# adaLN modulation in quarters, with packed weights and full-row score matmuls, in a hybrid SSD, MLA and PEER layer

## The reference

```python
ada = jnp.dot(jax.nn.silu(c), w_ada) + b_ada
shift1, scale1, gate1, shift2, scale2, gate2 = jnp.split(ada[:, None, :], 6, axis=-1)
h = layer_norm(x) * (1 + scale1) + shift1
z, xbc, dt_raw, q_a, kv_a, k_r, g_logits = jnp.split(jnp.dot(h, w_in), IN_OFFSETS, axis=-1)
...
scores = jnp.einsum('bqhd,bkhd->bhqk', q_blk, k).astype(jnp.float32) * scale
```

## Time and profile before

| | us |
|---|---|
| three runs | 3086.29, 3083.02, 3086.70 |
| median | 3086.29 |
| profiled execution, device time | 3086.24 |
| profiled execution, span of its instructions | 3084.3 |
| busy: PE, DVE, ACT, POOL | 1835.4, 2372.8, 684.8, 982.0 |
| low starts on PE (first matmul of unit 0) | 142.3 |
| att starts on PE | 209.6 |
| first gathered row used by DVE in PEER | 1709.3 |

### The profile page before, as it was taken

The page is one execution under the profiler, slowest core; times in us unless marked ns, Lnnn a source line. Parts: engine busy times, 40 slices in busy tenths (PEclk is TensorE's granted clock), DMA queues, the critical chain, the costliest instruction groups (busy, mean ns, idle before and its releaser), DMA issues.

```text
span 3084.3 us, 31543 instructions
## 1 busy us (share of the span) xinstructions
PE 1835.4 (60%) x10751; PEld 1496.0 (49%) x10751; DVE 2372.8 (77%) x2628; ACT 684.8 (22%) x712; POOL 982.0 (32%) x727
## 2 busy tenths in 40 slices
PE   1299999899999999999879221222222122122222
PEld 1288888888888888999769110111111010011111
DVE  7855556778878786444565898989898999999997
ACT  1143333234444444433343000000000000000000
POOL 0000001122222221000000555655554456666552
PEclk8598888999999999999989666566666556656666
DMA  7845556875666664655544999999999799999996
GB/s 271 308 148 162 167 176 207 286 222 191 209 207 201 202 213 159 239 184 185 210 144 131 376 404 416 392 401 391 403 389 407 309 403 406 418 404 400 404 405 266
DMA packets 255655, 880.19 MB, mean 285 GB/s; under 512 B 19496, under 2 KB 56976, under 8 KB 188208
## 3 DMA queue, kind: packets, MB, share of 16 engines
q0 software_dynamic: 93600, 614.51, 49.8%
q1 hardware_dynamic: 161872, 264.11, 25.9%
q10 hardware_dynamic: 64, 0.07, 0.0%
HBM read 876.49 MB, written 2.13 MB: 285 GB/s over the span
## 4 chain that ended last, share of the span: by engine, by line
PE 40%; DVE 29%; DMA 12%; issue 10%; POOL 5%; ACT 2%; SPq 0%; DVEq 0%; POOLq 0%; ACTq 0%
DVE ps L1822 10%; DMA rrow<-in_peer_u,eid 10%; PE ps L595 9%; PE ps L597 9%; PE ps L596 9%; POOL rrow L1956 5%; DVE acc L1312 4%; DVE rrow L1795 4%; PE ps L575 2%; PE ps L576 2%; PE ps L577 2%; DVE wlo L1256 2%; ACT whi L938 2%; DMA rrow<-in_peer_v,eid 1%; PE aux L794 1%
## 5 line engine op out<-in xcount | busy, mean ns | idle before, releaser
L918 PE MATMUL aux<-rrow,acc 128*128 128x512 f32 x512 | 333.6, 817 | 1021.5 <-DVE acc L1815 781.0
L1256 DVE TENSOR_TENSOR wlo<-raw,whi 128x2048 fp32r<-128x2048 f32 x216 | 508.7, 2355 | 404.5 <-ACT whi L938 392.1
L918 PEld LDWEIGHTS aux<-rrow,acc 128*128 128x128 f32 x512 | 131.3, 267 | 1223.2 <-issue 977.5
L1795 DVE CUSTOM_DVE_ANT_0 rrow<-rrow,h 128x2048 f32<-128x2048 f32 x256 | 582.3, 2291 | 63.2 <-DMA rrow<-in_peer_u,eid 44.4
L938 ACT ACTIVATE whi<-raw 128x2048 fp32r<-128x2048 f32 x216 | 413.2, 1913 | 816.4 <-PE ps L597 493.3
L1956 POOL DMA_INDIRECT rrow<-in_peer_u,eid x256 | 409.7, 1600 | 309.7 <-DVE eid L1747 90.1
L1956 POOL DMA_INDIRECT rrow<-in_peer_v,eid x256 | 358.4, 1400 | 361.5 <-DVE ps L1822 294.4
L1822 DVE SCALAR_TENSOR_TENSOR ps<-rrow,wgt,ps 128x2048 f32<-128x2048 f32 x192 | 452.2, 2355 | 14.4 <-DMA rrow<-in_peer_v,eid 6.7
L595 PE MATMUL ps<-h_hi,whi 128*128 128x256 f32 (+1 forms) x1568 | 457.8, 292 | 8.9 <-DVE wlo L1256 5.8
L596 PE MATMUL ps<-h_lo,whi 128*128 128x256 f32 (+1 forms) x1568 | 448.0, 286 | 0.0
L597 PE MATMUL ps<-h_hi,wlo 128*128 128x256 f32 (+1 forms) x1568 | 447.6, 285 | 0.0
(11 more groups left out here) (303 smaller groups left out, 2998.2 us busy)
## 6 DMA issues: line engine op xcount, KB each, us to landing
raw<-in_w_in SPq DMA_DIRECT2D x120, 1024.0 KB, 5.2
ada_in<-in_w_ada POOLq DMA_DIRECT2D x128, 512.0 KB, 5.1
ada_in<-in_w_ada SPq DMA_DIRECT2D x32, 1024.0 KB, 5.2
raw<-in_w_ssd_out SPq DMA_DIRECT2D x32, 1024.0 KB, 5.1
raw<-in_w_mla_out SPq DMA_DIRECT2D x16, 1024.0 KB, 7.1
raw<-in_w_mix_out SPq DMA_DIRECT2D x16, 1024.0 KB, 5.2
raw<-in_peer_w_q SPq DMA_DIRECT2D x16, 1024.0 KB, 5.1
raw<-in_w_ukv SPq DMA_DIRECT2D x8, 1024.0 KB, 5.4
```

The source lines that it names most:

```text
L918: last = mm(aux[:, n, :], diag[:, j // 2, j % 2, :], rrow[:, r % ROWS, n * W:n * W + W], start=(first and k == 0 and j == 0), stop=False, ...
L1256: V.tensor_tensor(wlo[:, n % 2, :, 0:cols_], raw[:, n % 4, :, 0:cols_], whi[:, n % 2, :, 0:cols_].bitcast(F32), ALU.subtract).then_inc(lo_ ...
L1795: last = V.tensor_tensor_reduce(row, row, h2[:, b, :], 1.0, 0.0, ALU.mult, ALU.add, dots[:, k, e:e + 1])
```

## The change

The weights are laid out anew on the host, without arithmetic, so that each 1 MB unit is one contiguous block and a partition's part of it one piece of 8 KB (`packed`, `unit`); POOL's halves are pieces of 4 KB. The first third of `w_ada` is regrouped into four quarters: a quarter holds the 512 shift and the 512 scale columns that belong to the same 512 channels, as eight chunks of 2 x 128 rows by 1024 columns. DVE adds up seven of the eight chunks of a quarter in 14 steps of 128x1024; PE multiplies the eighth directly with `csil` (16 one-column matmuls, `ada1_rest`) and adds DVE's sum (8 more, `ada1_sums`). Chunks go through five buffers.

`c` is also loaded by itself (`crow`) and turned before the other parameters; the small loads are issued by ACT instead of SP, and SP issues the constants, five chunks, and then x. DVE does quarter 0 before the copies of the parameters and the LayerNorm of x. The first six units of low are loaded within the loop over the quarters, in the order in which a quarter of h meets both slabs (unit 2q and 2q+1). DVE makes quarter q-1 of h, and `wlo` of its two units, after three chunks of quarter q, and the last quarter after all chunks. PE runs a quarter's two units as soon as they are ready, and the next quarter's `ada1_rest` behind them. The rope angles come after the last quarter of h, the sines later still; the q_a norm is no longer beside the kv_a units; both follow unit 6 and unit 7.

`kpeT` becomes two copies, each with zeros in the 64 partitions that a head does not use, so that the rope matmul of the scores has 128 rows; the mask matmul takes all 128 rows of the constants, of which 127 are zero in that place.

```diff
+QUARTERS, ADA_V, ADA_BUFS = 4, 7, 5
...
+        ada1_acc = at("ada1_acc", 110 * KB, [P, 2, 2 * W])
+        ada_in4 = at("ada_in4", 118 * KB, [P, 4, W])
+        crow = at("crow", 157 * KB, [DC, P])
+        def ada1_in(n):
+            t = ada_in4[:, :, :] if n % ADA_BUFS == 4 else ada_in[:, n % ADA_BUFS]
+            return t.rearrange("p a b -> p (a b)")
...
-        kpeT = at("kpeT", 125 * KB, [P, SEQ])
+        kpeT = at("kpeT", 124 * KB, [P, 2, SEQ])
...
+        def unit(name, u, kcs=4):
+            return a[name][ds(u * P, P), :].rearrange("p (kc n) -> p kc n", kc=kcs)
...
+            sp_.dma_start(con[:, :], a["consts"]).then_inc(con_in, 16)
...
+            def ada1_chunk(q, j):
+                n = 8 * q + j
+                if n >= ADA_BUFS:
+                    q0, j0 = divmod(n - ADA_BUFS, 8)
+                    if j0 < ADA_V:
+                        sp_.wait_ge(ada_used, q0 * ADA_V + j0 + 1)
+                    else:
+                        sp_.wait_ge(ada_pe_used, q0 * (8 - ADA_V) + j0 - ADA_V + 1)
+                sp_.dma_start(ada1_in(n), a["p_ada1"][ds(n * P, P), :]).then_inc(ada_full[n % ADA_BUFS], 16)
+            for q in range(QUARTERS):
+                for j in range(8):
+                    ada1_chunk(q, j)
+                    if q == 0 and j == ADA_BUFS - 1:
+                        for b in range(BLK):
+                            sp_.dma_start(x_in[:, b, :], a["x"][0, b * P:(b + 1) * P, :]).then_inc(x_loaded, 16)
+                    if q and j == 0:
+                        for s in range(2):
+                            load(U_LOW, 2 * (q - 1) + s, 0, 0, unit("p_in", S_LOW * 4 + 4 * s + q - 1))
...
+                for s in range(2):
+                    load(U_LOW, 6 + s, 0, 0, unit("p_in", S_LOW * 4 + 4 * s + 3))
+                for k in range(2):
+                    load(U_LOW, 8 + k, 0, 0, unit("p_dk", k, DC))
...
+            pe.wait_ge(con_in, 16)
+            pe.wait_ge(c_in, 16)
+            nc.tensor.transpose(aux[:, 2, 0:DC], crow[:, :], ident[0:DC, 0:DC]).then_inc(c_turned, 1)
+            pe.wait_ge(params_in, 16 * 17)
...
+            ada_sum = aux[:, 3, :]
+            def ada1_rest(q):
+                for j in range(ADA_V, 8):
+                    n = 8 * q + j
+                    pe.wait_ge(ada_full[n % ADA_BUFS], 16 * (n // ADA_BUFS + 1))
+                    for kc in range(2):
+                        for t in range(8):
+                            c = t * P
+                            last = mm(ada_sum[:, 8 * q + t:8 * q + t + 1],
+                                      ada1_in(n)[:, 2 * W * kc + c:2 * W * kc + c + P],
+                                      csil[:, 2 * j + kc:2 * j + kc + 1], start=(j == ADA_V and kc == 0 and t == 0),
+                                      stop=False, skip_group_check=True)
+                    last.then_inc(ada_pe_used, 1)
+            def ada1_sums(q):
+                pe.wait_ge(acc_ready, q + 1)
+                for t in range(8):
+                    last = mm(ada_sum[:, 8 * q + t:8 * q + t + 1], ada1_acc[:, q % 2, t * P:t * P + P],
+                              con[:, C_ONE:C_ONE + 1], start=False, stop=True, skip_group_check=True)
+                last.then_inc(acc_summed, 1)
+            pe.wait_ge(c_ready, 1)
+            ada1_rest(0)
+            ada1_sums(0)
...
-                for s in range(2):
-                    for q in range(4):
-                        if s == 0:
-                            pe.wait_ge(h_ready, q + 1)
-                        token_unit(U_LOW, 4 * s + q, 0, 0, h_hi, h_lo, 4 * q, DC - 1,
+                for q in range(QUARTERS):
+                    pe.wait_ge(h_ready, q + 1)
+                    for s in range(2):
+                        token_unit(U_LOW, 2 * q + s, 0, 0, h_hi, h_lo, 4 * q, DC - 1,
                                    [ps[:, s, b, :] for b in range(BLK)])
-                        if (s, q) == (1, 2):
-                            turn_cn(0)
+                    if q + 1 < QUARTERS:
+                        ada1_rest(q + 1)
+                        ada1_sums(q + 1)
                 for k in range(2):
                     channel_unit(U_LOW, 8 + k, 0, 0, h_hi, h_lo, 0, DC - 1,
                                  [(ps[0:64, 0, k, 0:SEQ], 0, True)], kcs=DC, width=64)
-                    if k == 0:
-                        turn_cn(1)
+                    turn_cn(k)
+                pe.wait_ge(cn_split, 1)
...
-                        r = slice(64 * (h % 2), 64 * (h % 2) + 64)
                         for b in range(BLK):
                             nk = P * (b + 1)
                             o = aux[:, h, b * P:b * P + nk]
                             t = slice(b * P, b * P + P)
                             mm(o, qn[:, h, t], kn[:, h, 0:nk], start=True, stop=False)
-                            mm(o, qpeT[r, h // 2, t], kpeT[r, 0:nk], start=False, stop=False)
-                            last = mm(o, con[0:1, C_MQ:C_MQ + P], con[0:1, C_MK + 256 - nk:C_MK + 256],
+                            mm(o, qpeT[:, h // 2, t], kpeT[:, h % 2, 0:nk], start=False, stop=False)
+                            last = mm(o, con[:, C_MQ:C_MQ + P], con[:, C_MK + 256 - nk:C_MK + 256],
                                       start=False, stop=True)
...
-            act.wait_ge(cols_ready, 1)
-            F(csil[:, :], cols[:, PC_C:PC_C + DC], ACT.Silu).then_inc(c_ready, 1)
-            act.wait_ge(params_in, 16 * 18)
+            def small_in(dst, src):
+                nc.scalar.dma_start(dst, src).then_inc(params_in, 16)
+            nc.scalar.dma_start(crow[:, :], rowsof(a["c"], 0, DC)).then_inc(c_in, 16)
...
+            act.wait_ge(c_turned, 1)
+            F(csil[:, :], aux[:, 2, 0:DC], ACT.Silu).then_inc(c_ready, 1)
+            act.wait_ge(params_in, 16 * 17)
...
-            for u in range(2):
-                hi(U_LOW, u, 0, 0)
-            for q in range(4):
+                  psf[:, 1024 * (r % 2):1024 * (r % 2) + 1024], ACT.Copy).then_inc(xT_ready, 1)
+            for q in range(QUARTERS):
                 act.wait_ge(h_full, q + 1)
                 F(h_hi[:, 4 * q:4 * q + 4, :], xnT[:, 4 * q:4 * q + 4, :], ACT.Copy).then_inc(h_hi_ready, 1)
+                for s in range(2):
+                    hi(U_LOW, 2 * q + s, 0, 0)
...
+                slab_done(U_LOW, 6, 0, 0)
                 sumsq(0)
-                for u in (6, 7):
-                    hi(U_LOW, u, 0, 0)
                 hi_flat(U_LOW, 8, 0, 0, DC * 64)
-                split_cn(0, PC_QN, cqT_hi)
-                hi_flat(U_LOW, 9, 0, 0, DC * 64)
                 slab_done(U_LOW, 7, 0, 0)
                 sumsq(1)
+                hi_flat(U_LOW, 9, 0, 0, DC * 64)
+                act.wait_ge(angles_ready, 1)
+                for k, tab_ in enumerate((sin2, cos2)):
+                    for e in range(2):
+                        F(tab_[:, :, 32 * e:32 * e + 32], angs[:, k], ACT.Sin).then_inc(sines_ready, 1)
+                split_cn(0, PC_QN, cqT_hi)
...
-                F(kpeT[:, :], aux[:, 3, 0:SEQ], ACT.Copy).then_inc(kpe_read, 1)
+                act.wait_ge(kpe_zero, 2)
+                F(kpeT[0:64, 0, :], aux[0:64, 3, 0:SEQ], ACT.Copy)
+                F(kpeT[64:P, 1, :], aux[64:P, 3, 0:SEQ], ACT.Copy).then_inc(kpe_read, 1)
...
+            def ada1_chunks(q, first, end):
+                if first == 0:
+                    dve.wait_ge(acc_summed, q + 1)
+                for j in range(first, end):
+                    n = 8 * q + j
+                    dve.wait_ge(ada_full[n % ADA_BUFS], 16 * (n // ADA_BUFS + 1))
+                    tile = ada1_in(n)
+                    acc_ = ada1_acc[:, q % 2, :]
+                    for kc in range(2):
+                        k = 2 * j + kc
+                        src = tile[:, 2 * W * kc:2 * W * kc + 2 * W]
+                        if k == 0:
+                            last = V.tensor_scalar(acc_, src, csil[:, k:k + 1], None, ALU.mult)
+                        else:
+                            last = V.scalar_tensor_tensor(acc_, src, csil[:, k:k + 1], acc_, ALU.mult, ALU.add)
+                        if kc == 0:
+                            link(last)
+                    if j < ADA_V - 1:
+                        last.then_inc(ada_used, 1)
+                        dve.wait_ge(ada_used, q * ADA_V + j + 1)
+                    else:
+                        last.then_inc(acc_ready, 1)
+                        dve.wait_ge(acc_ready, q + 1)
                         dve.sem_inc(ada_used, 1)
+            def h_quarter(q):
+                dve.wait_ge(acc_summed, q + 3)
+                link(V.tensor_tensor(adacol[:, 4 * q:4 * q + 4], aux[:, 3, 8 * q:8 * q + 4],
+                                     cols[:, PC_ADA + 4 * q:PC_ADA + 4 * q + 4], ALU.add))
+                link(V.scalar_tensor_tensor(adacol[:, DC + 4 * q:DC + 4 * q + 4], aux[:, 3, 8 * q + 4:8 * q + 8], 1.0,
+                                            cols[:, PC_ADA + DC + 4 * q:PC_ADA + DC + 4 * q + 4], ALU.add, ALU.add))
```

(59 more changed lines are left out.)

174 lines of the change are left out of this document (53 added, 121 removed).

## The result

Four runs of the changed kernel took 3004.59, 2998.77, 2994.73 and 3004.16 us, a median of 3001.47, against 3086.49 for four runs of the kernel before: ratio 0.9722, 95% interval 0.9701 to 0.9743, so faster. A later series on one chip gave 3005.53 for it (0.9732, 0.9716 to 0.9749). The forecast was 3022 with a range of 3006 to 3050; the change gains some 20 us more than that.

What follows compares the result with a forecast made beforehand. It took the setup (DVE and DMA busy), PE's low clock in the scores, and from 1760 us the gather transfers, which the change leaves alone, as limits; 3086.24 - 29.3 (setup) - 35 (scores) = 3022 us, range 3006 to 3050.

Steps and rivals of the forecast that it cites:

- Part 1: Modulation sums on DVE in the setup: 1.315 us a step, 17.9 a quarter, 71.5 us for four against 103 before.
- Part 2: Start of the setup: small loads moved to ACT let DVE's first sum begin at 10.7 us instead of 17.24.
- Part 3: DVE chain in the setup: 127.6 us plus waits of 7.6 for chunks and 8.1 for PE's sums, unit 6 at 143.3.
- Part 4: Stretch from unit 6 to att: 37.0 us against 31.4 before, so att starts at 180.3, 29.3 us earlier.
- Part 5: Score matmuls in att's four trips: full rows hold PE's clock at 2.4 GHz, gaining 35 us (bounds 0 and 37).
- Part 6: Everything else, packed units and POOL's 4 KB pieces and later start: costed at nothing, bound -8 to +3 us.
- The scores did not stay cold: Rival for att's scores: PE's clock stays low there, only the setup's gain counts, 3057 us; chance 0.10.
- Packing does not quicken the chunks: Rival for the setup: chunks come at 325 GB/s, 3.2 us each, waits grow by 13, 3035 us; chance 0.11 with other late starts.
- The slower case: Rival: PE's bursts between the setup's blocks stay at 1.2 GHz, att 9.4 us later, scores cold, 3096 us; chance 0.03.

Runs made afterwards that it cites:

- e2: The changed kernel with only the mask matmul of the scores back on one row, rope part still on 128 rows: 3015.24 us (ratio to before 0.9778).
- e3: The changed kernel with only the rope matmul of the scores back on 64 rows, mask still on 128 rows: 3014.77 us (ratio to before 0.9779).
- e5: The kernel before with only kpeT in two zero-padded copies and rope part and mask on 128 rows: 3037.16 us against 3085.35 (0.9845).
- e1: The changed kernel with the old score matmuls, rope part on 64 rows and mask on one row: 3055.21 us (ratio to before 0.9906).
- e11: The changed kernel with score matmuls grouped by kind, rope part on 128 rows, mask on one row: 3007.02 us (ratio to before 0.9747).
- e7: The changed kernel with all weights from att on, and POOL's part of w_ada, loaded from the original matrices: 3002.89 us (ratio to before 0.9735).
- e6: The changed kernel with only the 32 chunks of w_ada's first third loaded from the original matrix in 2 KB pieces: 3005.44 us (0.9738).

## Why the prediction was wrong

**Part 1, the sums: right.** A step cost 1.317 us where 1.315 was taken, the first of a quarter 0.75 to 0.79 where 0.78; a quarter is 32.24 - 11.23 less 3.16 of waits, 17.85, where 17.9 was taken.

**Part 2, the start: right,** 11.2 for 10.7. What ACT's 17 issues cost lay elsewhere: the last was out at 9.2 us and landed 25.9 us later, beside the stream of chunks. PE waits for it and DVE for PE, 3.85 us. I had costed the moved loads up to `csil` and not up to their next user.

**Part 3, the chain up to unit 6:** 145.8 for 143.3. Chunk waits were 8.1 in all (7.6), PE's last sums 6.3 (8.1), and the 3.85 were missing.

**Part 4, from unit 6 to att:** 36.1 us (145.8 to 181.9) for 37.0. The setup's gain is 27.7 for 29.3.

**Part 5, the scores: the step that failed.** Its words were "the 30 us windows shrink by 30 x (0.34 + 0.28 + 0.34 + 0.28) = 37.2; matmuls of 256 columns gain a little less than half, so 35": the scores' loss taken as that of the clock alone. Measured it is 51.7. The term that was missing is the 24 changes of the number of rows, 0.20 us each even at 2.4 GHz: 4.8 us a trip, 19 us in all. e2 and e3 measure it without the clock (3.13 us a trip for 16), e5 measures the whole (48.2 us). What is left for the clock, by difference, is some 32 of the 35. The evidence was there: the timeline of PE in the first 3.8 us of the scores, where the granted clock was still 1.00 and matmuls of 256 columns nevertheless stood 0.63 us apart, and PEld's 10.25 us of 19.3 in that stretch. I had read the clock's windows and the start of the fall and not the distances of the matmuls ahead of it. What was right is the direction: zero rows hold the clock as data rows do, and PE remained the limit when it sped up.

The Trainium skill has the missing rule, on a page that I had not weighed: "TensorEngine Tiling (Array Packing)", "Key Properties", says that changing the tiling mode drains TensorE, and its "Available Configurations" lists modes of 128, 64 and 32 rows. The trace agrees as far as it goes: at a change of rows the next weight load no longer starts beside the running matmul, and a change costs 0.20 us at 2.4 GHz. The page gives no figure. The rule that I set against this part (the Trainium skill, "TensorE: Matmul & The Clock Gate", "What's actually happening", where the half clock comes after an idle window) does not agree with e1 and e11, where PE is recorded as busy in the whole stretch and the clock falls.

**Part 6, the rest: right** within its bound; packed weights behind the setup give nothing that e7 can tell from the spread.

**The rivals.** The scores did not stay cold. "Packing does not quicken the chunks" was priced at 13 us from the 325 GB/s of the earlier trace rows. e6's profile puts it at some 3 us, less than the runs can tell from nothing. The 325 was DVE's own pace, not that of the pieces: four units, 4.19 MB, in 16 steps of 0.807 us are 325 GB/s, and e6 shows such pieces, with x among them, at 365. Why the DMA share read 0.98 beside a consumer that set the pace is not settled. So the packing is worth little here. By the sum of the parts the setup's 27.7 us come from the longer steps on DVE, PE's eighth, the earlier start and low beside the sums; no run took these apart. The slower case did not come either; PE's clock in the setup was 0.74 in the mean.

The sum is wrong in the main by one term: 3022 less 16.7 for the scores, plus 1.6 for the setup, less 2.2 for the rest, are 3004.7, the profiled execution. That this lies so near the range's lower end, 3006, is luck: that end was reckoned from waits in the setup that would be missing, and they were all there (part 3).
